# Shifted stream of an RWKV-7 mixer: one PSUM bank for each tile, halves summed into SBUF, shares scaled by ScalarE and added by GpSimd

## What is computed

```python
def token_shift(z, mu):
    prev = jnp.pad(z, ((0, 0), (1, 0), (0, 0)))[:, :-1]
    return z + (prev - z) * mu

def hybrid_mixer(h, positions, w_in, ...):
    proj = h @ w_in
    aw, rs = 3 * ATTN_WIDTH, RWKV_STREAM
    gates = jax.nn.sigmoid(proj[..., aw + rs:] + gate_bias)
    y_attn = dilated_attention(proj[..., :aw], positions) @ attn_w_up
    y_rwkv = rwkv7_time_mix(token_shift(proj[..., aw:aw + rs], rwkv_mu), ...)
    merged = gates[..., :D_MODEL] * y_attn + gates[..., D_MODEL:] * y_rwkv
    return merged @ w_o
```

## Time and profile before

| | us |
|---|---|
| median of 3 timed runs | 1862.27 (1862.12 to 1863.1) |
| profiled execution, time | 1873.29 |
| profiled execution, span from first to last instruction | 1871.5 |
| PE busy in it | 1844.7 |
| VectorE busy | 1181.7 |
| ScalarE busy | 1029.5 |
| GpSimd busy | 89.4 |
| mean granted clock of TensorE | 0.992 |

### The profile page before, as it was taken

One profiled execution on the slowest core, in us unless ns is written; L12 is line 12 of the kernel. 1 busy time (PEld: TensorE's weight loads), 2 busy tenths in 40 slices (PEclk: granted clock), 3 DMA queues, 4 the chain that ended last, 5 costly groups with the idle time before them and its releaser, 6 DMA issues.

```text
span 1871.5 us, 31118 instructions
## 1 busy us (share of the span) xinstructions
PE 1844.7 (99%) x12714; PEld 1570.5 (84%) x12714; DVE 1181.7 (63%) x2432; ACT 1029.5 (55%) x2127; POOL 89.4 (5%) x186
## 2 busy tenths in 40 slices
PE   8999999999999999999999999999999999999998
PEld 7888888888787888888888887888888888878887
DVE  5666545767655567665766664667566767566565
ACT  5565555644433555555655665556455656655554
POOL 0000000211210000010001000000000000000000
PEclk9999999999979999999999999999999999999999
DMA  6555443222214456535652333556355623334552
GB/s 245 181 204 234 160 156 113 103 86 73 97 53 161 136 191 227 201 113 186 238 194 85 133 134 113 189 211 231 112 184 209 235 98 133 136 113 169 202 186 107
DMA packets 42718, 296.30 MB, mean 158 GB/s; under 512 B 4832, under 2 KB 4960, under 8 KB 10576
## 3 DMA queue, kind: packets, MB, share of 16 engines
q1 hardware_dynamic: 41184, 288.48, 43.1%
q0 software_dynamic: 1392, 5.83, 0.9%
HBM read 293.25 MB, written 1.05 MB: 157 GB/s over the span
## 4 chain that ended last, share of the span: by engine, by line
PE 91%; DVE 4%; ACT 3%; DMA 1%; issue 1%; POOL 1%; SPq 0%; POOLq 0%; DVEq 0%; ACTq 0%
PE PS L1865 22%; PE PS L1807 16%; PE PS L1809 15%; PE PS L1808 15%; PE PS L1867 11%; PE PS L1816 1%; PE PS L2108 1%; DVE wlo L2742 1%; PE PS L2310 1%; PE PS L1842 1%; PE PS L2222 1%; PE PS L2089 1%; PE PS L2274 1%; PE PS L2266 1%; PE PS L2101 1%
## 5 line engine op out<-in xcount | busy, mean ns | idle before, releaser
L2742 DVE TENSOR_TENSOR wlo<-raw,whi 128x512 fp32r<-128x512 f32 (+5 forms) x788 | 612.4, 823 | 191.4 <-ACT whi L2353 184.6
L1865 PE MATMUL PS<-xhl,whi 128*128 128x512 f32 x1728 | 612.6, 398 | 0.0
L2353 ACT ACTIVATE whi<-raw 128x512 fp32r<-128x512 f32 (+5 forms) x788 | 531.6, 731 | 140.1 <-PE PS L1809 140.0
L1867 PE MATMUL PS<-xhl,wlo 128*128 128x256 f32 x1728 | 484.7, 280 | 0.0
L1865 PEld LDWEIGHTS PS<-xhl,whi 128*128 128x128 f32 x1728 | 324.6, 188 | 78.9
L1867 PEld LDWEIGHTS PS<-xhl,wlo 128*128 128x128 f32 x1728 | 326.2, 189 | 2.1
L1807 PE MATMUL PS<-whi,yh 128*128 128x512 f32 (+2 forms) x572 | 225.8, 395 | 0.4 <-DVE yl L3127 0.3
L1808 PE MATMUL PS<-wlo,yh 128*128 128x512 f32 (+2 forms) x572 | 222.4, 389 | 0.0
L1809 PE MATMUL PS<-whi,yl 128*128 128x512 f32 (+2 forms) x572 | 222.4, 389 | 0.0
L1807 PE MATMUL PS<-whi,xhl 128*128 128x512 f32 (+4 forms) x480 | 191.4, 399 | 0.3 <-DVE wlo L2742 0.3
L2827 DVE TENSOR_TENSOR arena<-arena,PS 128x256 f32<-128x256 f32 x216 | 90.3, 418 | 159.1 <-ACT arena L2423 159.1
(11 more groups left out here) (268 smaller groups left out, 2405.4 us busy)
## 6 DMA issues: line engine op xcount, KB each, us to landing
raw<-wall SPq DMA_DIRECT2D x249, 1024.0 KB, 4.8
raw<-wall SPq DMA_DIRECT2D x12, 768.0 KB, 4.2
raw<-wall SPq DMA_DIRECT2D x8, 968.0 KB, 4.7
raw<-wall SPq DMA_DIRECT2D x4, 896.0 KB, 4.5
arena<-ebias POOLq DMA_DIRECT2D x2, 768.0 KB, 5.1
raw<-wall SPq DMA_DIRECT2D x2, 720.0 KB, 4.2
raw<-wall SPq DMA_DIRECT2D x2, 640.0 KB, 3.7
X<-x SPq DMA_DIRECT2D x2, 512.0 KB, 6.1
```

What stands on the lines that cost most here:

```text
L1865: e.matmul(b, hi[:, c0:c0 + 128], xhl[:, k, :, :].rearrange("p a t -> p (a t)"), start=(k == 0), stop=False, skip_group_check=True)
L1867: p = e.matmul(b[:, 0:256], lo[:, c0:c0 + 128], xh[:, k, :], start=False, stop=(k == 7), skip_group_check=True)
L2353: e.activation(whi[slot_of(i)][:, c].bitcast(F32R), raw[i % 3][:, c], copy).then_inc(*M.sig("whi", ("split", i, q)))
L2742: e.tensor_tensor(wlo[slot_of(i)][:, c], raw[i % 3][:, c], whi[slot_of(i)][:, c].bitcast(F32), ALU.subtract).then_inc(*M.sig("wlo", *[("ha ...
```

## The change

shift takes a bank for each tile. Its matmuls get the form of the gate and up products: whi with the 512 columns of xhl, wlo with the 256 of xh. So the bank holds two halves to be summed. A new step shift_low (ScalarE) copies the upper half into one of two new SBUF tiles (ZS), and shift_sum (VectorE) adds the lower half of the bank; with that the bank is free. shift_copy (ScalarE) now reads this SBUF tile and writes the tile times 1 - mu, and a second instruction scales the SBUF tile by mu in place, behind a wait for the first. shift_mix moves to GpSimd and is an add of two SBUF tiles. All readers of the mixed tiles wait for GpSimd now. shift_low of a tile waits until the add of the tile two before it is done. In the planner, the step after a tile's matmuls no longer waits for the evacuation (self.ready = free), and the next pair starts without it (self.ready = self.now); up waits for five free banks. Paces and the table of fills have new values.

```diff
 PACE = {
-    "shift_mm": (("pe", 1.54),), "shift_copy": (("act", 0.7),), "shift_mix": (("dve", 0.86),),
+    "shift_mm": (("pe", 1.48),), "shift_low": (("act", 0.33),), "shift_sum": (("dve", 0.42),),
+    "shift_copy": (("act", 0.66),), "shift_mix": (("pool", 0.9),),
...
 BLANKS = {
-    ('turn_x', 1, 0, 0): 4, ('proj', 1, 'gate', 0, 0): 13, ('att_qk', 1, 0): 15, ('att_out', 1, 3, 0): 8,
-    ('r_vb', 1, 0): 14, ('r_d', 1, 4, 1): 7, ('r_dm0', 1, 5): 6, ('r_s', 1, 4, 3): 4, ('r_g0', 1, 7): 9,
-    ('r_d', 1, 7, 4): 5, ('r_d', 1, 7, 5): 4, ('r_s', 1, 7, 1): 4, ('r_s', 1, 7, 2): 3, ('r_s', 1, 7, 3): 3,
-    ('r_mean', 1, 7): 4, ('r_var', 1, 7): 7, ('r_turn2', 1, 7): 6, ('wout', 1, 3, 1, 0): 19,
-    ('turn_merged', 1, 4, 0): 4, ('wo', 1, 1, 0, 1): 7, ('proj', 4, 'gh', 0, 0): 20, ('turn_x', 5, 0, 0): 4,
...
+    ('proj', 0, 'gh', 0, 4): 4, ('turn_x', 1, 0, 0): 4, ('proj', 1, 'qkv', 1, 0): 6, ('proj', 1, 'qkv', 1, 4): 4,
+    ('proj', 1, 'gate', 0, 0): 13, ('att_qk', 1, 0): 15, ('att_out', 1, 3, 0): 8, ('r_wide', 1, 0): 8,
+    ('r_vb', 1, 0): 11, ('r_vb', 1, 1): 8, ('r_vb', 1, 2): 10, ('r_x', 1, 2, 4): 8, ('r_s', 1, 1, 2): 4,
+    ('r_d', 1, 3, 1): 6, ('r_yp', 1, 3): 3, ('r_d', 1, 5, 2): 6, ('r_var', 1, 5): 4, ('r_x', 1, 6, 5): 6,
+    ('r_s', 1, 6, 1): 4, ('r_s', 1, 6, 2): 4, ('r_s', 1, 6, 3): 4, ('r_w', 1, 7): 4, ('wout', 1, 3, 0, 0): 13,
+    ('r_s', 1, 7, 2): 4, ('r_s', 1, 7, 3): 4, ('r_mean', 1, 7): 3, ('r_turn2', 1, 7): 14, ('wout', 1, 3, 1, 0): 19,
+    ('turn_merged', 1, 4, 0): 4, ('wo', 1, 1, 0, 1): 3, ('wo', 1, 3, 0, 0): 8, ('proj', 4, 'gh', 0, 0): 20,
...
     def shift(self, s, sid, key, n, w):
-        yield from self.room(1)
-        self.bank.take(sid)
+
+
         i = self.take(*key)
         for j in range(n):
+            yield from self.room(1)
+            self.bank.take(sid + (j,))
             for k in range(0, 8, 4):
                 self.do("shift_mm", s, sid, j, k, i, n, w, (j, k) == (n - 1, 4))
                 self.pump()
-                if (j, k) != (n - 1, 4):
+                if (j, k) == (n - 1, 4):
+                    self.done(i)
+                elif k == 0:
                     yield 1
-        self.done(i)
-        self.do("shift_copy", s, sid, n, w)
-        yield 1
-        self.do("shift_mix", s, sid, n, w)
-        self.bank.give(sid)
-        yield 1
+            free = self.now
+            self.do("shift_low", s, sid, j, w)
+            self.do("shift_sum", s, sid, j, w)
+            self.bank.give(sid + (j,))
+            self.do("shift_copy", s, sid, j, w)
+            self.do("shift_mix", s, sid, j, w)
+            if j < n - 1:
+                self.ready = free
+            yield 1
...
             for q in "kvr":
                 yield from self.shift(s, (q, G), ("mix1", q, G), 2, 128)
                 self.did(q, G)
+                self.ready = self.now
...
                 if what == "up":
+                    yield from self.room(5)
                     self.acc(s, "up")
...
                 for k in range(k0, k0 + 4):
...
-                    p = mm3(b[0:w, j * 256:(j + 1) * 256], hi[:, c0:c0 + w], lo[:, c0:c0 + w], xh[:, k, :],
-                            xl[:, k, :], k == 0, k == 7)
-                if end:
-                    p.then_inc(*M.sig("pe", ("shift", sid), ("use", i)))
...
+                    e.matmul(b[0:w, :], hi[:, c0:c0 + w], xhl[:, k, :, :].rearrange("p a t -> p (a t)"), start=(k == 0),
+                             stop=False, skip_group_check=True)
+                    p = e.matmul(b[0:w, 0:256], lo[:, c0:c0 + w], xh[:, k, :], start=False, stop=(k == 7),
+                                 skip_group_check=True)
+                if k0:
+                    p.then_inc(*M.sig("pe", ("shift", sid, j), *[("use", i)] * end))
...
+            def shift_low(s, sid, j, w):
+                for t in due(("pe", ("shift", sid, j)), *marked("norm", 1), *summed_free(sid, j)):
+                    e.wait_ge(*t)
+                e.activation(summed(sid, j)[0:w], bank(sid + (j,))[0:w, 256:512], copy).then_inc(
+                    *M.sig("act", ("low", sid, j)))
+
+            def shift_copy(s, sid, j, w):
+                for t in due(("dve", ("sum", sid, j)), ("dve", ("less",)), *kzv_free(sid), COLS):
+                    e.wait_ge(*t)
+                z = summed(sid, j)[0:w]
+                e.activation(dest(sid)[0:w, j, :], z, copy, scale=less(mus(sid)[j])[0:w]).then_inc(
+                    *M.sig("act", ("share", sid, j)))
+                for t in due(("act", ("share", sid, j))):
+                    e.wait_ge(*t)
+                e.activation(z, z, copy, scale=col("mu", mus(sid)[j])[0:w]).then_inc(*M.sig("act", ("shift", sid, j)))
...
+            def shift_sum(s, sid, j, w):
+                b = bank(sid + (j,))
+                for t in due(("act", ("low", sid, j))):
+                    e.wait_ge(*t)
+                e.tensor_tensor(summed(sid, j)[0:w], summed(sid, j)[0:w], b[0:w, 0:256], ALU.add).then_inc(
+                    *M.sig("dve", ("sum", sid, j), ("free", sid + (j,))))
...
+            def shift_mix(s, sid, j, w):
+                o = dest(sid)[0:w, j, 1:256]
+                for t in due(("act", ("shift", sid, j))):
+                    e.wait_ge(*t)
+                e.tensor_tensor(o, o, summed(sid, j)[0:w, 0:255], ALU.add).then_inc(
+                    *M.sig("pool", ("mix", sid), ("mixed", sid, j)))
```

More of the change, by code:

```diff
@@ L558, in do @@
         ready, read = self.ready, self.weights_of(step)
-        if step[0] in ("shift_copy", "gate_attn", "resid", "proj_out", "in2_out"):
+        if step[0] in ("shift_low", "gate_attn", "resid", "proj_out", "in2_out"):
             ready += HOP["pe"]
@@ L1583, in build @@
         LW = sp.take(1024)
+        ZS = [sp.take(256) for _ in range(2)]
         sp = Space()
@@ L1731, in kzv_free, with tile_no, summed, summed_free @@
             return marked("kzv", sid[1] - 2) if sid[1] >= 2 else marked("attn", 1) if sid[1] else marked("norm", 1)
+        def tile_no(sid, j):
+            return 2 * sid[1] + j if sid[0] == "l" else 3 + 6 * sid[1] + 2 * "kvr".index(sid[0]) + j
+        def summed(sid, j):
+            return ZS[tile_no(sid, j) % 2]
+        def summed_free(sid, j):
+            n = tile_no(sid, j) - 2
+            if n < 0:
+                return []
+            old = (("l", n // 2), n % 2) if n < 3 else (("kvr"[(n - 3) % 6 // 2], (n - 3) // 6), (n - 3) % 2)
+            return [("act", ("shift",) + old), ("pool", ("mixed",) + old)]
         def less(j):
@@ L2015, in r_vb @@
                 b = bank(("r_vb", g))
-                for t in due(bank_free(("r_vb", g)), ("dve", ("mix", ("v", g // 2))), ("dve", ("bt", g))):
+                for t in due(bank_free(("r_vb", g)), ("pool", ("mix", ("v", g // 2))), ("dve", ("bt", g))):
                     e.wait_ge(*t)
@@ L2455, in in2_out @@
                 i.then_inc(*M.sig("act", tile, ("free", tile)))
-            def shift_copy(s, sid, n, w):
-                o, b = dest(sid), bank(sid)
-                for t in due(("pe", ("shift", sid)), ("dve", ("less",)), *kzv_free(sid)):
+            def shift_low(s, sid, j, w):
+                for t in due(("pe", ("shift", sid, j)), *marked("norm", 1), *summed_free(sid, j)):
                     e.wait_ge(*t)
-                for j in range(n):
-                    e.activation(o[0:w, j, :], b[0:w, j * 256:(j + 1) * 256], copy, scale=less(mus(sid)[j])[0:w]).then_inc(
-                        *M.sig("act", ("shift", sid)))
+                e.activation(summed(sid, j)[0:w], bank(sid + (j,))[0:w, 256:512], copy).then_inc(
[9 more added lines that the diff above has]
+                e.activation(z, z, copy, scale=col("mu", mus(sid)[j])[0:w]).then_inc(*M.sig("act", ("shift", sid, j)))
             def lora_act(s):
-                for t in due(("dve", ("mix", ("l", 1)))):
+                for t in due(("pool", ("mix", ("l", 1)))):
                     e.wait_ge(*t)
@@ L2512, in r_square @@
                 k3 = KZV[g // 2 % 2]["k"][:, g % 2, :]
-                for t in due(*front_free(g), ("dve", ("mix", ("k", g // 2))), COLS):
+                for t in due(*front_free(g), ("pool", ("mix", ("k", g // 2))), COLS):
                     e.wait_ge(*t)
@@ L2718, in scalar_program @@
             run("act", {"still": still_, "out": out_, "split": split, "sumsq": sumsq, "scale": scale, "turn_x": turn_x, "glu": glu,
-                        "proj_out": proj_out, "shift_copy": shift_copy, "lora_act": lora_act, "att_qk": att_qk,
+                        "proj_out": proj_out, "shift_low": shift_low, "shift_copy": shift_copy,
+                        "lora_act": lora_act, "att_qk": att_qk,
                         "att_soft": att_soft, "att_turn": att_turn, "turn_ao": turn_ao, "turn_merged": turn_merged,
@@ L2858, in m1_begin @@
                     *M.sig("dve", ("less",)))
-            def shift_mix(s, sid, n, w):
-                o, b = dest(sid), bank(sid)
-                for t in due(("act", ("shift", sid)), COLS):
```

(11 more changed lines are left out.)

18 lines of the change are left out of this document (10 added, 8 removed).

## The result

The changed kernel takes 1876.01 us (median of 4 runs, 1875.28 to 1876.65), the kernel before beside it 1862.68. The ratio is 1.0066, with a 95% interval of 1.005 to 1.0081. That is 13.3 us or 0.7% slower, clear of the interval, and outside the forecast range of 1856.0 to 1871.0. The profiled execution took 1876.12 us, with a span of 1874.1 and a mean clock of 0.998; unlike the one of before it has no dip between 340 and 600 us, so it can be set beside the timed runs directly.

A forecast was written before the change was run, and what follows sets the result against it. PE's work, its idle time and the fills were taken to bound the kernel. Matmuls -1.6, lead +1.2, fills +2.0 and 0 sum to +1.6 us: 1863.9 for the median, range 1856.0 to 1871.0.

The forecast's parts named there:

- Bound, and the dip of the profiled run: Whole kernel: PE's work, idle time and fills bound it; a 21 us half-speed dip explains nearly all of 11.0 us.
- Matmuls, -1.6: Shifted tiles: two matmuls per k instead of three, 0.3525 for 0.360 us, saving 1.6 us (0 to 3.2).
- Lead, +1.2 (0.5 to 2): Start of stage 1: longer evacuation delays the casts for qkv 1 by 0.9 us; ten new fills agree; +1.2 us.
- Evacuation, 0: Shifted tiles outside the lead: a pair's result comes 1.1 us later, but waits for mixes and banks cost nothing.
- the price of lost cover: Behind the other 12 pairs: if PE's remaining queue no longer covered the later mixes, 13 us at most.
- Fills, +2.0 and 0: Stage 1: 23 more fills where the rwkv part begins cost 2.0 us; 33 later ones fit under idle time, 0.
- (1): Later rwkv part and stage 0: PE reaches the fills with work at hand and they are paid; 1868.4 us, chance 0.16.
- (2): Port shared by VectorE and GpSimd: adds hold VectorE's two-input operations; +3.5 us, 1867.4, chance 0.05.
- (3): Pairs up to k 2 of the rwkv part: next tile planned earlier, up to 5.3 us; 1858.6, chance 0.15.
- (4): Clock: a dip enters the timed runs (1873.2, chance 0.05) or new fills end an existing one (1854.6, chance 0.08).
- (5): Whole kernel: nothing moves, as the third weight load was hidden and the waits stay; 1862.3 us, chance 0.01.
- What I named as fatal: Closing remark: wrong above all if the plan moved groups by more than these microseconds, or the clock differs.

The follow-up runs named there:

- after_short_evac: The changed kernel with the old evacuation (one scaled ScalarE copy, one VectorE mix per tile; upper half left out of the result); 1871.2 us.
- before_new_fills: The kernel before with the changed kernel's table of fills and nothing else changed; 1872.8 us against 1862.7.
- after_free_stream: The changed kernel with its planner letting the stream go on right after its matmuls, instructions and paces the same; 1890.5 us.
- after_old_fills: The changed kernel with the table of fills of the kernel before, 266 for 336; 1885.5 us.
- before_pace: The kernel before with one planner number changed, the pace of shift_mm from 1.54 to 1.48; 1875.0 us (1863.2 beside it).
- short_evac_old_fills: The changed kernel with the old evacuation (upper half left out of the result) and the old table of fills; 1879.4 us against 1863.5 beside it.

## Where the prediction was right and wrong

**Bound, and the dip of the profiled run.** Right in the main. A second profile of before and the clocks of its timed runs show that the dip of the earlier trace rows is not in most timed runs, though a shorter one can be. Adding the difference to both bases was sound; the difference was wrong.

**Matmuls, -1.6.** The spacing came out as forecast; the gain in time is not shown. PE's timeline at the end of the l part; the rows left out are the same pair again:

```profile
221.51 0.39 PE L1955 MATMUL PS<-xhl,whi 128*128 128x512 f32 x1
...
223.25 0.39 PE L1955 MATMUL PS<-xhl,whi 128*128 128x512 f32 x1
223.48 0.28 PE L1957 MATMUL PS<-xhl,wlo 128*128 128x256 f32 x1
223.60 0.87 PE L1843 MATMUL PS<-still 128*128 128x256 f32 x6
225.05 0.50 PE L1834 MATMUL PS<-whi,xhl 128*128 128x512 f32 x1 [0.59 <-DVE wlo L2779]
```

(223.25 - 221.51) / 5 = 0.348 per k, for 0.360 in the earlier trace rows and 0.3525 forecast from the earlier trace rows. In a group of four k in the woven part it is 0.35 to 0.36 (339.55 below and the two starts behind it, 339.90 and 340.26). By this spacing the 216 pairs save 0 to 2.6 us, and -1.6 lies between. That after_short_evac is 1.6 faster than before_new_fills is no proof of it: the plan differs as well, and the scatter is as large.

**Lead, +1.2 (0.5 to 2).** Price low, inside the bounds. The last row above: PE waits 0.59 us behind the six fills, where it was 0.16 with none; qkv 1 begins 225.05 - 223.60 = 1.45 us after the fills did. The scalings and the handovers were mis-sized. ScalarE's rows behind the last pair, for the earlier trace rows:

```profile
221.02 0.38 ACT L2488 ACTIVATE arena<-PS 128x256 f32<-128x256 f32 x1 [0.24 <-PE PS L1957]
221.97 0.51 ACT L2495 ACTIVATE arena<-arena,small 128x256 f32<-128x256 f32 x1 [0.57 <-DVE arena L2901]
222.51 0.51 ACT L2499 ACTIVATE arena<-arena,C 128x256 f32<-128x256 f32 x1
222.93 2.18 ACT L2381 ACTIVATE whi<-raw 128x512 fp32r<-128x512 f32 x4
```

A scaled copy from SBUF takes 0.51, not 0.42; the row that I took the earlier trace rows is a tanh without a scale, on 64 partitions. The casts start 1.9 us after the copy, not 1.6: each instruction also begins a little after the end of the one that it waits for, 0.1 us and more from the copy to the sum (221.53, on VectorE). From stage 0's end to the last sum of gates 0 and 1 the stretch grew by 2.0 us (104.4 to 106.4), and 0.5 of that remains with the old evacuation (104.9). That is the upper end of my bounds.

**Evacuation, 0.** This step failed too, by 4.8 us. Its length was not what I had wrong. The add was cheaper than I took it to be. All 27:

```profile
L3362 POOL TENSOR_TENSOR arena<-arena x27: 721/734/1214, 220.3 to 477.4; 128x255 f32<-128x255 f32 x27
```

The usual one takes 0.73 us, for 1.15 forecast, and the whole chain from the copy at 221.02 to the end of its add (223.10, 0.75) 2.83 us, for 2.8. What failed is the cover. I counted instructions on engines with idle time and found one waiter for the mixes in the trace of before, but that trace tells who waited with the old order and lengths. Against the short evacuation the profile of after is longer by 1.5 us in the lead, 1.4 in the attention part and 0.8 in the middle. (It is 0.6 longer in stage 0 as well, where both have the same instructions; so that much is scatter.) Only lora_act is shown as waiting for GpSimd, for 0.9 us; by which steps the rest reaches PE is not shown. The 12 x 1.1 = 13 us that I gave as the price of lost cover should have stood in the range in part; I left it out of the sum's bounds altogether.

**Fills, +2.0 and 0, and nothing for the plan.** This is the step that failed most. The sum had 2.0 us for 23 fills at the beginning of the rwkv part, 0 for the 33 behind them, and no term at all for the new order. On the old plan the table costs 10.1. The middle stretch, with the 23 and ten of the 33, grew by 4.8 there. I had set the 4.0 us of the 33 against 5.4 us of idle time from 340 to 600 and said that they fit under it. That compares two totals: a fill covers a wait only where it stands ahead of it and PE reaches it early. And it was the idle time of the old plan. The new plan has other waits, 14.0 us from 340 to 600 for 6.2, and costs 15.9 us with the old fills and the old evacuation; the new fills bring that down by 8.2 and not further. For the start of the recurrence the rows are, for the earlier trace rows:

```profile
338.68 0.58 PE L2023 MATMUL PS<-C,arena 128*128 128x2 f32 x4 [0.63 <-ACT arena L2551]
...
339.55 0.40 PE L1955 MATMUL PS<-xhl,whi 128*128 128x512 f32 x1
...
340.61 1.10 PE L1843 MATMUL PS<-still 128*128 128x256 f32 x8
...
343.50 1.47 PE L1843 MATMUL PS<-still 128*128 128x256 f32 x11
345.42 0.99 PE L2029 MATMUL PS<-C,arena 128*128 128x128 f32 x6 [0.46 <-DVE arena L3039]
```

8 and 11 fills, and still 0.46 us of wait behind them, where 14 fills left 0.40 before. Five fills more did not end this wait.

**The rivals.** (1), the fills paid, 1868.4: right in its mechanism on the old plan, at 4.5 us of a measured 10.1. For the changed kernel its condition, that the waits stay where they were, does not hold. (2), the port: its mechanism is real, its price of 3.5 us is not confirmed. Two places of GpSimd's timeline, and the same two of VectorE's:

```profile
349.88 0.83 POOL L3362 TENSOR_TENSOR arena<-arena 128x255 f32<-128x255 f32 x1 [3.90 <-ACT arena L2499]
...
477.40 1.21 POOL L3362 TENSOR_TENSOR arena<-arena 128x255 f32<-128x255 f32 x1 [0.21 <-ACT arena L2499]
```

```profile
350.02 1.23 DVE L2779 TENSOR_TENSOR wlo<-raw,whi 128x512 fp32r<-128x512 f32 x1
...
477.34 0.69 DVE L2779 TENSOR_TENSOR wlo<-raw,whi 128x512 fp32r<-128x512 f32 x1
```

The add at 477.40 began 0.06 us after VectorE's subtraction of two SBUF tiles and took 1.21 for its usual 0.73; the subtraction at 350.02 began 0.14 us after an add and took 1.23 for 0.69. In these two places either side is held while the other runs. By the rule of the Trainium skill (SBUF — State Buffer, "SBUF: two separate sides") each blocks the other; the subtraction at 350.02 shows the direction that the trace of before did not. But it is rare. Of the 27 adds five took 0.83 us or more, together 1.3 us over the usual length, and the mean of VectorE's 128x512 subtraction over the whole trace went only from 686 to 691 ns (472 of them), 2.4 us of VectorE in all. How much of that reaches PE is not shown. After the mix went back to VectorE 3.6 us were gained, by the shorter chain or by the freed port; no run parts these two. (3), the stream runs ahead, 1858.6: its premise was wrong, and so was my account of the change above. Within a pair the planner goes on at once, but behind the pair it still holds the dense chain until the expected mix, now 0.3 + 0.33 + 0.1 + 0.42 + 0.1 + 0.66 + 0.1 + 0.9 + 0.15 = 3.1 us for 2.1. I read the branch for j < n - 1 as if it held for both tiles. And where the stream did run ahead (after_free_stream), the kernel was 14.5 us slower. (4), the clock: the changed kernel has no dip in this stage, so none was added; without the new fills there would have been some (after_old_fills). (5): no.

**What I named as fatal** was a plan that moves groups against each other by more than these microseconds. before_pace (12 us) and short_evac_old_fills (15.9) show what another order can cost. I had it as a remark at the end and gave it no chance and no term. It should have been the widest term of the range.

**What stays open.** How the 4.8 us of the evacuation divide among single waits; what the new matmuls and the bank for each tile are worth on the old plan; which steps the new order moved to make its 8 us of waits; and what a plan and fills fitted to the changed evacuation would reach. The other plans that I tried were all worse, but none had fills fitted to it.

## What to carry to other kernels

Where a planner writes the order and a table of fills belongs to it, a local change is also a new plan: price it first as "this kernel with a disturbed plan", here 10 us and more for one pace changed by 4%, and only then by its own instructions. Do not set the length of added fills against total idle time; look at each fill's place and ask whether PE would arrive there early. Do not take an engine that is busy for 58% of the time as free: an instruction on the chain that others wait for can cost time wherever the order leaves no slack. And measure a table of fills on the plan that it is meant for: this one costs 10.1 us on one order and gives 9.5 on another.

## What the runs showed of the hardware

The dips of the granted clock to its lower level lasted 3.4, 6.8, 10.2, 17 and about 21 us in these traces, and each costs at most half its length. A GpSimd add of two 128x255 float32 tiles takes 0.73 us, less than the 1.15 of its one-input tensor_scalar on 128x256 with a scalar for each partition; with constants, one on 128x512 takes 0.62. A ScalarE copy of 128x256 from PSUM takes 0.38 us plain (L2488) and 0.47 with a scale for each partition (L2462 of the kernel before, median of 27); from SBUF, with such a scale, it takes 0.51 (L2495).
